# Gated layer: value panels 3 to 6 in two pairs of seven block products, with the weight sums on GpSimd

## The reference, cut to what matters

```python
SG_FF = 6 * D_MODEL
SG_HALF = SG_FF // 2            # 3072
...
def chunked_spatial_gating(h, w_in, v_gain, w_s, b_s, w_out):
    z = jax.nn.gelu(h @ w_in, approximate=False)
    u, v = jnp.split(z, 2, axis=-1)
    v = rms_norm(v, v_gain).reshape(B, nw, SG_WINDOW, SG_GROUPS, SG_HALF // SG_GROUPS)
    ...
    vm = jnp.einsum('gij,bnjgc->bnigc', w, v) + b_s.T.astype(v.dtype)[None, None, :, :, None]
    return (u * vm.reshape(B, S, SG_HALF)) @ w_out
```

## Time and profile before

| what | value |
|---|---|
| median of three timed runs | 1805.95 us (1805.54 to 1808.11) |
| profiled execution, first to last instruction | 1804.1 us |
| its mean granted TensorE clock | 0.995 |
| TensorE, VectorE, ScalarE, GpSimd busy | 1743.7, 1174.8, 666.0, 101.1 us |
| value panels 2 to 6 on TensorE | 691.25 to 800.1 us of the span |
| mixing begins | 805.4 us |

### The profile page before, as it was taken

How to read it: one execution, slowest core, us unless ns; L and a number is a source line. 1 busy time by engine, 2 the same in 40 slices (tenths; PEclk the granted TensorE clock), 3 DMA queues, 4 the chain that set the end, 5 groups by cost and what they waited for, 6 DMA issues and landing times.

```text
span 1804.1 us, 24298 instructions
## 1 busy us (share of the span) xinstructions
PE 1743.7 (97%) x9361; PEld 1440.3 (80%) x9361; DVE 1174.8 (65%) x2441; ACT 666.0 (37%) x1081; POOL 101.1 (6%) x194
## 2 busy tenths in 40 slices
PE   4999999999999999999999999999999999989999
PEld 3877769888888888888888898888888887766787
DVE  7778766876376656565454558874687478656564
ACT  4324673523242333233132335232323342366512
POOL 0001100001000100100000000010001100000000
PEclk9999999999999999999999999999999999999999
DMA  9355324335433634652423224354335322300351
GB/s 376 117 184 184 112 72 158 120 138 172 141 117 117 190 119 157 208 181 70 153 81 140 92 84 156 131 167 169 130 138 179 137 94 92 130 36 24 147 193 47
DMA packets 45471, 245.98 MB, mean 136 GB/s; under 512 B 6256, under 2 KB 6480, under 8 KB 27440
## 3 DMA queue, kind: packets, MB, share of 16 engines
q1 hardware_dynamic: 24848, 155.36, 24.0%
q0 software_dynamic: 20512, 89.11, 14.8%
HBM read 229.23 MB, written 15.22 MB: 135 GB/s over the span
## 4 chain that ended last, share of the span: by engine, by line
PE 80%; DVE 12%; ACT 4%; issue 2%; DMA 2%; DVEq 0%; SPq 0%; ACTq 0%
PE ps L476 69%; DVE w_lo L1517 3%; DMA ada_raw<-in_ada 1%; PE ps L840 1%; ACT w_hi L1088 1%; DVE ada_raw L1541 1%; PE ps L973 1%; DVE ada_first L1902 1%; PE ps L651 1%; DVE pre L1634 1%; PE ps L660 1%; PE ps L674 1%; PE ps L962 1%; PE ps L998 1%; PE ps L953 1%
## 5 line engine op out<-in xcount | busy, mean ns | idle before, releaser
L1517 DVE TENSOR_TENSOR w_lo<-w_raw,w_hi 128x2048 fp32r<-128x2048 f32 x136 | 311.6, 2291 | 137.3 <-ACT w_hi L1088 137.1
L1088 ACT ACTIVATE w_hi<-w_raw 128x2048 fp32r<-128x2048 f32 x136 | 260.1, 1913 | 354.3 <-PE ps L476 329.2
L476 PE MATMUL ps<-h_hi,w_hi 128*128 128x512 f32 (+1 forms) x1008 | 378.2, 375 | 5.2 <-DVE w_lo L1517 3.3
L476 PE MATMUL ps<-h_lo,w_hi 128*128 128x512 f32 (+1 forms) x1008 | 372.7, 370 | 0.0
L476 PE MATMUL ps<-h_hi,w_lo 128*128 128x512 f32 (+1 forms) x1008 | 372.5, 370 | 0.0
L476 PEld LDWEIGHTS ps<-h_hi,w_hi 128*128 128x128 f32 x1008 | 190.2, 189 | 39.8 <-issue 4.5
L476 PEld LDWEIGHTS ps<-h_hi,w_lo 128*128 128x128 f32 x1008 | 190.1, 189 | 32.1
L476 PEld LDWEIGHTS ps<-h_lo,w_hi 128*128 128x128 f32 x1008 | 190.3, 189 | 30.2
L476 PE MATMUL ps<-hid_hi,w_hi 128*128 128x512 f32 (+1 forms) x576 | 211.6, 367 | 0.0
L476 PE MATMUL ps<-hid_hi,w_lo 128*128 128x512 f32 (+1 forms) x576 | 210.9, 366 | 0.0
L476 PE MATMUL ps<-hid_lo,w_hi 128*128 128x512 f32 (+1 forms) x576 | 210.9, 366 | 0.0
(11 more groups left out here) (391 smaller groups left out, 2430.7 us busy)
## 6 DMA issues: line engine op xcount, KB each, us to landing
w_raw<-in_slabs SPq DMA_DIRECT2D x136, 1024.0 KB, 4.8
ada_raw<-in_ada POOLq DMA_DIRECT2D x104, 512.0 KB, 5.1
s_tables<-s_tab POOLq DMA_DIRECT2D x4, 2692.0 KB, 9.2
s_t<-s_tables POOLq DMA_DIRECT2D x4, 2692.0 KB, 9.8
ada_first<-in_ada SPq DMA_DIRECT2D x16, 512.0 KB, 15.1
a_bias<-in_a_bias POOLq DMA_DIRECT2D x16, 256.0 KB, 3.5
xT<-in_xT SPq DMA_DIRECT2D x4, 512.0 KB, 6.2
s_toeplitz<-KTp POOLq DMA_DIRECT2D x32, 64.0 KB, 3.2
```

The costliest lines, as they stand in the source:

```text
L476: last = mm(o, l, r, start=start and n == 0, stop=stop and n == 2)
L1088: A(w_hi[s][:], w_raw[:, s, :], ACT.Copy).then_inc(sem("hi_done"), 1)
L1517: tt(w_lo[s][:], w_raw[:, s, :], w_hi[s][:].bitcast(F32), ALU.subtract).then_inc(sem("lo_done"), 1)
```

## The change

Panels 1 and 2 stay as they are. Panels 3 and 4, and 5 and 6, are each made as a 2 x 2 block product C = A B: A is the input (rows: tokens 0-255 and 256-511; columns: k 0-511 and 512-1023), B two panels of weights; each block of B is one slab. Seven products of blocks take the place of eight. A product is one slab against 256 tokens: 2 x 4 x 3 = 24 matmuls of 128 x 512. In the text they are P0 to P6, with their slab operands 11, 21, t2, t1, t3, 22, t4, where t3 = 22 - 12, t2 = t3 + 11, t1 = 22 - t2, t4 = 21 - t2.

- GpSimd makes the four t sums of each pair (`weight_sum`), in place in the raw buffers, each a subtract or add of 128 x 2048; two more raw buffers are laid over `b_ws` and `ada_raw`.
- ScalarE and VectorE split seven operands for each pair, not four slabs.
- VectorE makes whole parts and four sums of the input in the first two panels (`whole`, `made`) and their `lo`, ScalarE their `hi`.
- The partial results are kept in `b_v` by ScalarE (`keep`), and added to by VectorE. ScalarE takes 12 of the 16 sums of squares of panels 3 to 6, by `Square` with an accumulator, directly behind each gelu.
- The `ada` tiles move from the panels into the u phase and the products behind it (`ADA_U`, `ADA_DOWN`). The loads of `b_ws` and `b_bs`, and of these tiles, move behind the sums in GpSimd's queue; SP's loads of the two pairs are written out.

```diff
+OPERAND = "11", "21", "t2", "t1", "t3", "22", "t4"
+PAIR_BUFS = (0, 1, 2, 3), (3, 1, 2, 0)
...
@@ gpsimd
+            def weight_sum(pair, i):
+                raw11, raw21, raw12, raw22 = (st_raw[b] for b in PAIR_BUFS[pair])
+                if i == 0:
+                    for name in ("12", "22"):
+                        gp.wait_ge(sem(LOADS[pair][name][0]), LOADS[pair][name][1])
+                    ins = gp.tensor_tensor(raw12, raw22, raw12, ALU.subtract)
+                elif i == 1:
+                    gp.wait_ge(sem("lo_done"), S_PAIRS + PRODUCTS * pair + 1)
+                    ins = gp.tensor_tensor(raw11, raw12, raw11, ALU.add)
+                elif i == 2:
+                    ins = gp.tensor_tensor(raw22, raw22, raw11, ALU.subtract)
+                else:
+                    gp.wait_ge(sem("lo_done"), S_PAIRS + PRODUCTS * pair + 2)
+                    ins = gp.tensor_tensor(raw21, raw21, raw11, ALU.subtract)
+                ins.then_inc(sem("w_sums"), 1)
+                gp.wait_ge(sem("w_sums"), 4 * pair + i + 1)
...
@@ tensor
+                product(0, x, h_part(0, 0), x_free)
+                product(1, y, h_part(4, 0), y_free)
+                product(2, x, sum_part(1), p1_kept)
+                product(3, z, sum_part(0), z_free)
+                product(4, x, sum_part(2), u2_kept)
+                product(5, z, sum_part(3), p5_kept)
+                product(6, x, h_part(4, 2), c22_done)
...
@@ scalar
+                split_product(pair, 5)
+                for t in range(2):
+                    keep(3, t, z, out_of(1, 1, t))
+                for t in range(2):
+                    act.wait_ge(sem("acc_free"), b0 + 1 + t)
+                    gelu(0, 0, t)
+                split_product(pair, 6)
+                for t in range(2):
+                    act.wait_ge(sem("st_c22"), 2 * pair + 1 + t)
+                    gelu(1, 1, t)
+                split_product(pair + 1, 0)
+                for t in range(2):
+                    act.wait_ge(sem("acc_free"), b0 + 3 + t)
+                    gelu(0, 1, t)
+                for t in range(2):
+                    filled(6, t)
+                    A(out_of(1, 0, t), x[t][:], ACT.Gelu).then_inc(sem("bv_done"), 1)
...
@@ vector, first panel
+            sq(0, 0)
+            sq(0, 1)
+            dve.wait_ge(sem("nlo"), KT * 2 * c.base("tails"))
+            step(whole(h_part21, 0, 1), whole(h_part22, 1, 1), whole(h_part11, 0, 0))
+            made(tt(sum_raw(0), h_part21, h_part22, ALU.add))
+            made(tt(sum_raw(1), sum_raw(0), h_part11, ALU.subtract))
+            split()
...
@@ vector, end of a pair
+                split_product(pair, 5)
+                split_product(pair, 6)
+                for t in range(2):
+                    dve.wait_ge(sem("st_kept"), 6 * pair + 5 + t)
+                    filled(4, t)
+                    tt(out_of(1, 1, t), x[t][:], out_of(1, 1, t), ALU.add).then_inc(sem("st_c22"), 1)
+                split_product(pair + 1, 0)
+                for t in range(2):
+                    dve.wait_ge(sem("st_kept"), 6 * pair + 3 + t)
+                    filled(5, t)
+                    free(tt(out_of(0, 1, t), z[t][:], out_of(0, 1, t), ALU.add))
...
-ADA_BV = 0, 4, 4, 5, 4, 4
+ADA_U = 2, 1, 1
+ADA_DOWN = 2, 2, 0
```

More of the change, by code:

```diff
@@ L827, in _ @@
             head_natural()
-            for _ in range(5):
+            for _ in range(BV_PLAIN - 1):
                 panel_natural()
+            for pair in range(BV_PAIRS):
+                panel_pair(pair)
             pe.wait_ge(sem("bws_masked"), 1)
@@ L1369, in _, with gelu_v @@
             act.wait_ge(sem("s5_stored"), 16 * (L + 1) * 2)
[L1370 to L1374, removed]
+            def gelu_v(p):
+                return lambda t, b: A(b_v[:, t, p * 512:(p + 1) * 512], b[:], ACT.Gelu).then_inc(sem("bv_done"), 1)
+            head()
+            c.add("slab")
+            for t in range(2):
+                gelu_v(0)(t, full(t, TT))
+            split()
+            high_sum(1, 2)
+            high_sum(0, 2)
+            for t in range(2, TT):
+                gelu_v(0)(t, full(t, TT))
+            c.add("slab")
+            split()
+            high_sum(2, 3)
+            high_sum(3, 4)
+            c.add("slab")
+            split_product(0, 0)
+            for t in range(TT):
+                gelu_v(1)(t, full(t, TT))
+            c.add("slab")
+            for pair in range(BV_PAIRS):
+                panel_pair(pair)
+            act.wait_ge(sem("red_done"), 5)
+            A(stat[:, 0:TT], stat[:, 0:TT], ACT.Sqrt, bias=eps[:], scale=1.0 / SG_HALF).then_inc(sem("std_done"), 1)
             for ch in range(CHUNKS):
@@ new lines, in square_v @@
+            def square_v(pair):
+                p, b0 = BV_PLAIN + 2 * pair, c.base("bank") - PAIR_BANKS[pair]
+                for t in range(2):
+                    dve.wait_ge(sem("bv_done"), TT * BV_PLAIN + 8 * pair + 6 + t + 1)
+                    v = b_v[:, 2 + t, p * 512:(p + 1) * 512]
+                    x = ps[(b0 + 4 + t) % 8]
+                    ins = V.tensor_tensor_reduce(out=x[:], in0=v, in1=v, scale=1.0, scalar=0.0, op0=ALU.mult, op1=ALU.add,
+                                                 accum_out=vss[:, 2 + t, p:p + 1])
+                    free(ins, 1 if t == 0 else PAIR_BANKS[pair] - 5)
@@ L2049, in _, with sq @@
             ffn(40, 0)
[L2052 to L2067, removed]
+            def sq(p, t):
+                b = full(t, TT)
+                dve.wait_ge(sem("bv_done"), TT * p + t + 1)
+                v = b_v[:, t, p * 512:(p + 1) * 512]
+                free(V.tensor_tensor_reduce(out=b[:], in0=v, in1=v, scale=1.0, scalar=0.0, op0=ALU.mult, op1=ALU.add,
+                                            accum_out=vss[:, t, p:p + 1]))
@@ new lines, in _ @@
+            head()
+            c.add("slab")
+            sq(0, 0)
[4 more added lines that the diff above has]
+            made(tt(sum_raw(1), sum_raw(0), h_part11, ALU.subtract))
+            split()
+            low_sum(1)
+            low_sum(0)
+            sq(0, 2)
+            sq(0, 3)
+            c.add("slab")
@@ new lines, in _ @@
+            split()
+            made(tt(sum_raw(2), h_part11, h_part21, ALU.subtract))
+            step(whole(h_part12, 1, 0))
+            made(tt(sum_raw(3), h_part12, sum_raw(1), ALU.subtract))
+            low_sum(2)
+            low_sum(3)
+            c.add("slab")
+            split_product(0, 0)
+            for t in range(TT):
+                sq(1, t)
+            c.add("slab")
+            for pair in range(BV_PAIRS):
+                panel_pair(pair)
+            dve.wait_ge(sem("bws_in"), 32)
@@ L2100, in _ @@
                     c.add("slab")
[L2101 to L2102 removed]
+                if ch != 1:
+                    ada_put()
+                (tail if ch == CHUNKS - 1 else residual)(64, lambda s: ada(ADA_DOWN[ch], 0))
+                if ch < CHUNKS - 1:
+                    ada_put()
             ffn(88, 1)
```

256 lines of the change are left out of this document (225 added, 31 removed).

## The result

The changed kernel takes 1824.8 us (median of four runs, 1823.18 to 1826.43) where the kernel before, measured beside it, takes 1805.74: ratio 1.0101, 95% interval 1.0088 to 1.0115, some 19 us slower. The direction was forecast, the time (1818.4, range to 1823.0) was not: it lies 1.8 us above the range.

The account below looks back on a forecast made before the run. TensorE, busy 97% of the span, was taken as the bound. 10.9 us saved against 14.3 lost in waits gave +3.4; exclusion by GpSimd's sums added 9.0: +12.4, so 1818.4 us, range 1806.5 to 1823.

Parts of the forecast that it names:

- Saving, 10.9 us: Both pairs: 168 matmuls each instead of 192, so 48 fewer at 0.2267 us, 10.9 us saved.
- First panel, 3.9 + 3.6 = 7.5: Panel 2's `lo` behind five VectorE instructions costs TensorE 3.9 us; the first pair's t3 sum holding a square adds 3.6.
- First pair under the sums, 1.7 + 1.3: First pair: t2 and t1 sums make the `lo` of P1 1.7 us late, t4 holds that of P2 1.3 more.
- First pair's end, 1.6 and 3.4 + 2.4: First pair's end: ScalarE's queue costs 1.6, then 3.4 us; second pair's t1 sum holds the `lo` of P1 2.4 more.
- Second pair's first wait, 1.6: End of the second pair: ScalarE's gelus and squares delay a `hi` and its `lo`, TensorE loses 1.6 us.
- Before the mixing, 3.8: Second pair's second wait: the mixing waits for the squares and the `scale_v` chain, 3.8 us lost.
- Price of a sum, 4.4: One GpSimd weight sum of 128 x 2048 takes 4.4 us, the middle of 3.5 and 5.2.
- exclusion at 0.6: Rival: a GpSimd sum and a VectorE instruction with two SBUF operands exclude each other entirely; +12.4 us, chance 0.60.
- +12.4: Net change in the kernel's time: +3.4 us without GpSimd's influence plus 9.0 from exclusion.
- 14.3 + 9.0: TensorE's forecast waits: 14.3 us at the first panel and pair ends from the queues, 9.0 more from exclusion by the sums.

Follow-up runs that it names:

- the three mended kernels: Changed kernel with sums on VectorE and queues reordered; then also the first mixing later; then also VectorE's queue finer: 1799.82, 1797.79, 1796.78 us.
- a1: Changed kernel with GpSimd's eight weight sums left out, each a one-column write instead (output not the reference's): 1811.56 us, ratio 1.0028.
- d1: Changed kernel with P0 of the first pair waiting for one freed bank less: 1824.27 us, one run.
- a2: Changed kernel with 28 and 24 extra matmuls put in front of the waits of 7.0 and 6.0 us: 1821.07 us, ratio 1.0084.
- b1: Changed kernel with the eight weight sums made by VectorE in its own queue, none by GpSimd: 1813.97 us, ratio 1.0048.
- c1: Changed kernel with GpSimd only writing zeros to a 128x2048 buffer in place of each sum: 1809.51 us, one run.
- e1: Kernel before the change, with the `lo` of panel 2's first half made four times so TensorE waits 6.2 us: 1814.18 us, ratio 1.0042.
- a4: Changed kernel with the next pair's two `hi` ahead of gelus on ScalarE, and TensorE's wait for `b_ws` moved to the mixing: 1817.10 us, ratio 1.0067.
- c2: Changed kernel with GpSimd multiplying one buffer by 2 in place of each sum: 1819.84 us, one run.

## Why the prediction was right and wrong

- **Saving, 10.9 us.** Right: less the 5.5, 2.9 and 1.5 us of waits that the three mended kernels have left, it gives 5.4, 8.0 and 9.4; measured are 5.3, 7.3 and 9.0.
- **First panel, 3.9 + 3.6 = 7.5.** Measured 7.0; a1 gives 4.1 of it to the queue, and the 2.9 that are left go to the sum.
- **First pair under the sums, 1.7 + 1.3.** Measured 1.7 + 1.3; the 1.7 showed as a bank, d1 shows the `lo` behind it.
- **First pair's end, 1.6 and 3.4 + 2.4.** Measured 1.1 and 6.0. A gelu with its square took 1.29 us, not 1.46.
- **Second pair's first wait, 1.6.** Misplaced: 3.0, ended by the memset of `b_ws`. The prediction costed the loads of `b_ws` and not the memset behind VectorE's adds, for which TensorE waits ahead of the u phase. The `lo` alone (813.29 + 2.29 = 815.58) would have made it 1.1; TensorE was ready at 814.53. VectorE's row:

```profile
816.95 0.48 DVE L2413 MEMSET b_ws<- 64x512 f32 x1 [0.16 <-issue]
```

- **Before the mixing, 3.8.** It didn't show: the 3.0 came first, and the half slab of 24 matmuls, eight of them at the lower clock, took 7.2 us instead of 5.4. Where the clock held, it was 1.4 to 1.5 (a2, b1, c1).
- **Price of a sum, 4.4, exclusion at 0.6.** The rival chosen was the right one, and the price near: 4.5 to 4.6 undisturbed. The 4497 ns of the Trainium skill ("GPSIMD Engine Reference", section 3.1) agrees with the shortest, 4.53.
- **The step that failed** is the sum "+12.4". It counted each wait as lost time and what follows at 0.2267 us a matmul, so TensorE's clock had no term in it. In all, the waits were 20.0 us where 23.3 were forecast (14.3 + 9.0). That alone would have given 9.1 net, 1815: the 3.3 us too many, 2.4 of them at the second pair's end, hid part of the missing term by luck. The clock took 7.3 us behind three of the waits, the first matmul behind each of the other four some 0.1 (0.34 to the next), and 1.6 us went at 675, ahead of the changed stretch, where the profiled execution of before has no fall and seven of the fourteen, e1's too, have one, so that it isn't the change's. 20.0 - 10.9 + 7.3 + 0.5 + 1.6 = 18.5. The span grew by 19.7; 0.6 of the rest is there before 655 us, and 0.6 I can't place; whatever the moved `ada` tiles cost, taken as nothing in the prediction, has no more room than that. a2 and e1 show the clock's term by itself.

## What to carry to other kernels

A wait of TensorE of several microseconds costs more than its length: add what the next matmuls lose at half the clock, and fill the wait with matmuls if it can't go, as a2 did. Work handed to GpSimd isn't free for VectorE if it reads SBUF: here the eight sums held VectorE for 15.8 us, nearly the 17.8 that it spends when it makes them itself, and one hold alone was 4.4 us, ahead of a `lo` that TensorE needed. When the same work is cut into pieces of half the length, walk each queue again: the gelus, squares and sums that were harmless ahead of a `lo` with 10.9 us between slabs were not with 5.4, and putting each `lo` and `hi` first, with the sums back on VectorE and the first mixing later, turned 19 us slower into 7 to 9 faster.

## What the runs showed of the hardware

- In the changed stretch, waits of 4.1 us and more (13 of them, over all runs) were each followed by a granted clock of 0.5, for 6 to 13 matmuls at 0.427 us, and waits of 2.2 and less by none. Of thirteen between 2.6 and 3.0 seven were, and one more in part (a4's, before the mixing: its eight matmuls of 128 columns and three behind them): why a wait of 2.95 is followed by it in the changed kernel and another of 2.95 isn't in b1 stays open. So does the fall at 675, behind a wait of 1.0 that all kernels have and seven of fourteen executions answer so.
- The fall need not come with the first matmul: behind the wait that ends at 817.49 the spacing is 0.227 until 819.05 and 0.43 from there.
- A GpSimd multiply by a constant, 128x2048 in fp32, takes 5.4 us where it begins beside no VectorE instruction, longer than a sum of two buffers (4.5 to 4.6), and lets a waiting VectorE instruction go 3.5 us in (c2). Which part of the instruction that is, no run shows.
